# Two decoder layers with a mixture of experts: weights moved in transfers of 2 MB instead of 1 MB, through a ring of 16 slots

## What is computed

```
z = h @ w_in                               # 1024 x 3076, heads: 12 dilated, 4 forgetting
y = concat(rms(dilated attention), rms(forgetting attention)) @ w_out
h = layer_norm(alpha * h + y)
probs = softmax(h @ w_router + b_router)   # 16 experts in 4 groups
# the best group, then the best 2 experts inside it, gates normalised
for every chosen expert e:
    a = silu(x @ w_gate[e]) * (x @ w_up[e]);  out += gate * (a @ w_down[e])
h = layer_norm(alpha * h + out)
```

## Time and profile before

| | us |
|---|---|
| median of three runs | 1417.3 |
| the profiled execution | 1413.33 |
| its span, first to last instruction | 1411.7 |
| PE busy | 1159.9 (82%) |
| VectorE busy | 295.4 (21%) |
| ScalarE busy | 181.0 (13%) |

### The profile page before, as it was taken

One profiled execution on the slowest core, in us unless ns is written; L12 is line 12 of the kernel. 1 busy time (PEld: TensorE's weight loads), 2 busy tenths in 40 slices (PEclk: granted clock), 3 DMA queues, 4 the chain that ended last, 5 costly groups with the idle time before them and its releaser, 6 DMA issues.

```text
span 1411.7 us, 17085 instructions
## 1 busy us (share of the span) xinstructions
PE 1159.9 (82%) x5948; PEld 556.2 (39%) x5949; DVE 295.4 (21%) x777; ACT 181.0 (13%) x407; POOL 4.6 (0%) x12
## 2 busy tenths in 40 slices
PE   7999967799987677777999895989999877567765
PEld 4456453334432323233445644434444323222322
DVE  1334241111111111113235324010202111111113
ACT  1044210001001000000105411000000010000100
POOL 0000000000000000000000000000000000000000
PEclk9999978999999899889799996899999998878998
DMA  9931129999999999999942121647888999999995
GB/s 365 394 120 61 60 90 368 382 417 422 422 421 422 421 422 421 422 423 419 414 148 94 60 92 59 233 146 261 341 357 330 422 422 421 422 421 422 422 421 218
DMA packets 62361, 444.72 MB, mean 315 GB/s; under 512 B 7152, under 2 KB 7408, under 8 KB 8944
## 3 DMA queue, kind: packets, MB, share of 16 engines
q1 hardware_dynamic: 61168, 439.97, 76.7%
q0 software_dynamic: 1152, 4.19, 0.8%
HBM read 443.08 MB, written 1.05 MB: 315 GB/s over the span
## 4 chain that ended last, share of the span: by engine, by line
PE 58%; DMA 30%; issue 6%; DVE 3%; SPq 2%; ACT 1%; DVEq 0%; ACTq 0%
DMA ring<-in_w_up_dram 22%; PE acc L668 12%; PE lo L586 9%; PE lo L486 9%; PE lo L474 8%; DMA ring<-in_w_down_dram 8%; PE acc L746 4%; PE lo L461 3%; SPq L319 2%; PE acc L540 1%; PE acc L391 1%; PE lo L382 1%; PE lo L759 1%; PE lo L437 1%; PE acc L643 1%
## 5 line engine op out<-in xcount | busy, mean ns | idle before, releaser
L486 PE MATMUL lo<-ring,z 128*32 128x512 f32 x2112 | 281.6, 671 | 148.0 <-DMA ring<-in_w_up_dram 107.6
L486 PEld LDWEIGHTS lo<-ring,z 128*32 128x32 f32 x2112 | 65.6, 120 | 343.1 <-issue 158.5
L668 PE MATMUL acc<-ring,actT 128*128 128x512 f32 x384 | 176.1, 616 | 1.5 <-ACT actT L832 1.5
L474 PE MATMUL lo<-ring,z 128*64 128x512 f32 x672 | 152.8, 609 | 24.6 <-issue 22.7
L461 PEld LDWEIGHTS lo<-z,h 128*128 128x128 f32 x1088 | 132.4, 196 | 55.2 <-issue 51.0
L461 PE MATMUL lo<-z,h 128*128 128x128 f32 x1088 | 148.7, 287 | 2.5 <-DVE z L1173 2.5
L586 PE MATMUL lo<-ring,z 128*128 128x512 f32 x288 | 129.2, 610 | 19.9 <-issue 19.9
L668 PEld LDWEIGHTS acc<-ring,actT 128*128 128x128 f32 x384 | 74.7, 199 | 90.5 <-issue 90.5
L474 PEld LDWEIGHTS lo<-ring,z 128*64 128x64 f32 x672 | 48.3, 140 | 123.9 <-issue 113.7
L586 PEld LDWEIGHTS lo<-ring,z 128*128 128x128 f32 x288 | 56.0, 197 | 90.3 <-issue 90.3
L935 ACT ACTIVATE z<-lo 64x512 f32<-64x512 f32 x22 | 13.1, 593 | 493.5 <-PE lo L486 493.5
(11 more groups left out here) (179 smaller groups left out, 712.3 us busy)
## 6 DMA issues: line engine op xcount, KB each, us to landing
ring<-in_w_gate_dram SPq DMA_DIRECT2D x128, 1024.0 KB, 15.9
ring<-in_w_up_dram SPq DMA_DIRECT2D x128, 1024.0 KB, 18.9
ring<-in_w_down_dram SPq DMA_DIRECT2D x128, 1024.0 KB, 25.0
ring<-in_w_in_dram SPq DMA_DIRECT2D x24, 1024.0 KB, 24.7
ring<-in_w_out_dram SPq DMA_DIRECT2D x8, 1024.0 KB, 30.3
ln_gb<-in_ln_dram POOLq DMA_DIRECT2D x8, 512.0 KB, 7.2
cst<-in_consts_dram SPq DMA_DIRECT2D x1, 1416.0 KB, 13.6
h<-in_x_dram SPq DMA_DIRECT2D x1, 1024.0 KB, 5.5
```

The lines of the kernel that those rows point to most:

```text
L474: mm = nc.tensor.matmul(lo[half * W:(half + 1) * W, bank, :], lhsT, ring[:, s, at:at + 512], start=start, stop=stop, skip_group_check=True)
L486: return nc.tensor.matmul(lo[at * T:(at + 1) * T, bank, :], lhsT, ring[:, s, col:col + 512], start=start, stop=stop, skip_group_check=True)
L668: mm = nc.tensor.matmul(acc[:, 2 + t, :], actT[:, k, t * P:(t + 1) * P], ring[:, 2 * c + k // 4, (k % 4) * CH:(k % 4 + 1) * CH], start=(k ...
```

## The change

The host lays the weights out so that 2 MB are contiguous, with 16 KB for each partition, and one transfer fills two neighbouring slots. SP waits for both slots to be free, and signals `ring_full` of the first of them alone. PE waits once for each pair. PE still frees each slot by itself, at the same instruction as before. The 416 weight transfers of 1 MB become 208 of 2 MB; bytes, order, slots and all arithmetic stay.

```diff
-    w_in = np.stack([slots_of(a["w_in"][:, :, c * CH:(c + 1) * CH], 4) for c in range(N_CH)], 1)
+    w_in = np.stack([slots_of(a["w_in"][:, :, c * CH:(c + 1) * CH], KB) for c in range(N_CH)], 1)
-    out = {"x": a["x"], "w_in": w_in, "w_out": slots_of(a["w_out"], 2),
-           "w_gate": slots_of(a["w_gate"], 2), "w_up": slots_of(a["w_up"], 2), "w_down": slots_of(a["w_down"], 2),
+    out = {"x": a["x"], "w_in": w_in, "w_out": slots_of(a["w_out"], 4),
+           "w_gate": slots_of(a["w_gate"], 4), "w_up": slots_of(a["w_up"], 4), "w_down": slots_of(a["w_down"], 4),
...
+            def two_slots(s):
+                return ring[:, s:s + 2, :].rearrange("p s n -> p (s n)")
...
             def load_matrix(layer, m, expert, first, turn):
-                for i in range(4):
-                    s = first + i
+                for i in range(2):
+                    s = first + 2 * i
                     sp.wait_ge(ring_free[s], turn)
+                    sp.wait_ge(ring_free[s + 1], turn)
                     src = expert_v[m][:, bass.ds(layer, 1), bass.ds(expert, 1), i, :]
-                    sp.dma_start(ring[:, s, :], src.rearrange("p l e f -> p (l e f)")).then_inc(ring_full[s], 16)
+                    sp.dma_start(two_slots(s), src.rearrange("p l e f -> p (l e f)")).then_inc(ring_full[s], 16)
...
             def tiny_gate_up(first, gate_full, full):
                 for i in range(4):
-                    pe.wait_ge(ring_full[first + i], gate_full)
-                    pe.wait_ge(ring_full[UP + i], full)
+                    if i % 2 == 0:
+                        pe.wait_ge(ring_full[first + i], gate_full)
+                        pe.wait_ge(ring_full[UP + i], full)
...
                 for s in range(4):
-                    pe.wait_ge(ring_full[DOWN + s], full)
+                    if s % 2 == 0:
+                        pe.wait_ge(ring_full[DOWN + s], full)
```

More of the change, by code:

```diff
@@ L333, in _ @@
                         sp.sem_inc(passed, 1)
[L334 to L340, removed]
+                    s = 2 * c
+                    for i in range(2):
+                        sp.wait_ge(ring_free[s + i], gate_turn if s < UP else turn)
+                    src = w_in_v[:, bass.ds(l, 1), c, 0, :]
+                    sp.dma_start(two_slots(s), src.rearrange("p l n -> p (l n)")).then_inc(ring_full[s], 16)
+                for q in range(2):
+                    s = ODD + 2 * q
+                    for i in range(2):
+                        sp.wait_ge(ring_free[s + i], gate_turn)
                     src = w_out_v[:, bass.ds(l, 1), q, :]
-                    sp.dma_start(ring[:, ODD + q, :], src.rearrange("p l n -> p (l n)")).then_inc(ring_full[ODD + q], 16)
+                    sp.dma_start(two_slots(s), src.rearrange("p l n -> p (l n)")).then_inc(ring_full[s], 16)
                 load_matrix(l, 0, 0, EVEN, sp.snap(gate_turn + 1))
@@ L557, in narrow_item @@
                 for i in range(4):
-                    if i >= 1:
+                    if i == 2:
                         pe.wait_ge(ring_full[UP + i], full)
@@ L665, in project @@
                 for k in ks:
-                    if t == 0 and k % 4 == 0:
-                        pe.wait_ge(ring_full[2 * c + k // 4], fulls[2 * c >= UP])
+                    if t == 0 and k == 0:
+                        pe.wait_ge(ring_full[2 * c], fulls[2 * c >= UP])
                     mm = nc.tensor.matmul(acc[:, 2 + t, :], actT[:, k, t * P:(t + 1) * P],
@@ L740, in _ @@
                     for k in range(KB):
-                        if t == 0 and k % 2 == 0:
+                        if t == 0 and k % 4 == 0:
                             pe.wait_ge(ring_full[ODD + k // 2], gate_full)
```

## The result

| | kernel before | changed kernel | ratio, 95% interval |
|---|---|---|---|
| first comparison, median us | 1415.5 | 1404.1 | 0.9918 (0.9895 to 0.9941) |
| second comparison, median us | 1413.8 | 1405.5 | 0.9936 (0.9914 to 0.9957) |
| profiled execution, us | 1413.3 | 1404.7 | |

The change makes the kernel 0.6 to 0.8% faster: the medians differ by 11.4 us in the first comparison (4 executions of each kernel) and by 8.3 in the second (21 before, 8 changed), where 7.5 were forecast. The second interval holds the forecast's 1409.8 / 1417.3 = 0.9947; the first ends 0.0006 short of it.

The account below looks back on a forecast made before the run. The weights' stream was taken to bound two stretches, with PE setting the time in others. -12.3 + 1.5 + 0.7 + 1.8 + 0.8 = -7.5 us, from the median of 1417.3 to 1409.8 us, range 1402 to 1420.

Parts of the forecast that it names:

- The rate: Both layers' weight streams: 10 ns per packet, 0.089 us saved per pair of slots, 138 pairs, -12.3 us.
- The store and x: Two other transfers used to estimate a packet's own time: 15 ns from the store, some 29 from the load of x.
- the constants: Their 11 KB rows, at 39.8 us per MB against the weights' 38.5, showed no gain from longer rows.
- The start: Where each layer's stream starts, the first pair waits for its second slot: +1.5 us in layer 0, +0.7 in layer 1.
- The start of the kernel: w_in's first two slots go out together at 3 us, before PE has its turned input: costs nothing.
- The end: Each layer's last down matrix: 16 products instead of 8 after the last landing, +0.9 us per layer, +1.8.
- Within an item: Paired waits and freeing inside a stream's items cost 0, unless a lower TensorE clock adds up to 3 us per layer.
- Code fetches: Two places in layer 0 where PE stands for code while DMA is full: longer packets delay it, +0.8 us (0 to 2).
- The sign for a wrong prediction: Wrong if the rate rises and the end of layer 0's experts doesn't move by some 3 us.
- that only signals go: Rival: hardware cuts 16 KB rows into two 8 KB packets, saving 1.4 us against 4.8; 1420.7 us, chance 0.08.
- that 16 KB rows stream worse: Rival: 16 KB rows go at the constants' rate, 138 pairs cost 23.5 us; 1445.6 us, mild form 1429, chance 0.10.
- the small packet time (a = 3.5 ns): Rival: a pair gains only 0.031 us, 4.3 us in all against 4.8 of losses; 1417.8 us, no change, chance 0.17.

Follow-up runs that it names:

- experiment 1: Changed kernel with its 2 MB transfers and paired waits, but in the old rows of 8 KB; 1418.1 us, 1.0033 against the kernel before.
- experiment 2: Kernel before with its 1 MB transfers, but SP and PE both wait for two slots at once; 1418.4 us, 1.0036.
- experiment 6: Changed kernel with gate and down matrices in transfers of 4 MB, up matrices in 2 MB; 1419.9 us, 1.0053 against the kernel before.
- second traces: Traces of two unchanged repeats: the changed kernel once more (ratio 0.9936) and the kernel before once more as a control (1.0000).
- experiment 10: Kernel before with 1 MB transfers and PE's waits per slot, only SP waits for two free slots; ratio 1.0000.
- experiment 7: Changed kernel with the last 2 MB of each layer's last down matrix as two 1 MB transfers, a wait for each; 1406.7 us, 0.9947 against the kernel before.
- experiment 4: Changed kernel with each 4 MB expert matrix in one transfer, rows of 32 KB, waits for four slots; 1447.6 us, 1.0254 against the kernel before.
- experiment 3: Kernel before with its 1 MB transfers and waits per slot, but in rows of 4 KB; 1431.8 us, 1.0130.
- experiment 8: Changed kernel with gate matrices in one transfer of 4 MB, up and down in 2 MB; 1412.3 us, 0.9980 against the kernel before.

## Why the prediction was right

**The rate, -12.3 forecast.** The term was right in kind and about a sixth too large: 0.075 us per pair (4.970 - 4.895) times 138 is -10.4. It can be read a second way, from the changed kernel's items against experiments 1 and 2, which lack its rows: -10.4 and -10.8. The chosen 10 ns per packet were 0.075 / 9 = 8.3 ns, with 9.4 from rows of 4 KB. The store and x were too high with 15 and 29, as suspected for their start, and the constants misleading on the other side.

The Trainium skill ("DMA: Bandwidth & Descriptors", "Where 436 GB/s comes from") puts the ceiling of the SBUF ports at 435 GB/s. The 428 GB/s of the changed kernel and the 431 of experiment 6 lie below it, so no run here shows a ceiling. The Trainium skill's rule of about 3 cycles beside a packet's bytes (same page, "Why small descriptors are slow (HBM only)"), by which an estimated 4 us would have been won against 4.8 of costs, is too small here: 8 KB against 16 KB rows differ by 1.5%, not 0.6%.

**The start, +1.5 and +0.7.** In layer 0 the first pair of the stream was issued at 279.0 and landed after 7.7 us:

```profile
L323 SPq DMA_DIRECT2D ring<-in_w_gate_dram x1: 333/333/333, 279.0 to 279.0; - x1
...
DMA to landing us min/median/max: 7.7/7.7/7.7
```

at 286.7, where 287.1 was forecast; but this execution reached its items 1.2 us earlier. Counted from the first item, the pair landed after 77.9 us and the second slot of the kernel before after 75.6: +2.3 us, where 1.5 were forecast (+2.2 between the second traces). 0.6 of the excess is the landing itself, 7.7 us for a lone pair instead of 4.7 + 2.4; the other 0.2 is PE, which freed the slot later. In layer 1 the pair landed 199.1 us after the first item, and the slot of the kernel before after 199.0:

```profile
L323 SPq DMA_DIRECT2D ring<-in_w_gate_dram x1: 333/333/333, 1067.9 to 1067.9; - x1
...
DMA to landing us min/median/max: 7.6/7.6/7.6
```

That is +0.1 (-0.4 between the second traces), where 0.7 were forecast. Experiment 10 says the same of SP's waits alone: 1.5 in layer 0, nothing in layer 1.

**The start of the kernel, 0.** This term was put at nothing, because w_in's first two slots go out together before PE has its turned input. In the changed kernel they land after PE has it. PE's first projection waits for the pair, where that of the kernel before waits for ScalarE:

```profile
12.93 14.00 PE L680 MATMUL acc<-ring,actT 128*128 128x512 f32 x32 [1.47 <-DMA ring<-in_w_in_dram]
...
12.47 13.99 PE L668 MATMUL acc<-ring,actT 128*128 128x512 f32 x32 [0.76 <-ACT actT L832]
```

The wait is 0.7 us longer (1.12 us in the second trace of the changed kernel, 0.4 longer). It lies outside the items.

**The end, +1.8.** 16 products in 1.92 us after the last wait in both layers instead of 8 in 1.06, as written: +1.7. Experiment 7 puts 8 of them before the last wait again and wins 1.2 and 0.7.

**Within an item, 0.** Held: the DMA share stayed 1.01 to the end of layer 0. What didn't hold is the sign that PE's total wait for DMA would shrink by the gain: it grew, by the pairing of the waits (experiment 2). Experiment 4 shows how near the edge is: with four slots the same wait costs 28 us.

**Code fetches, +0.8.** 7.77 and 7.46 us instead of 7.70 and 7.27 (the second of these from the same view as the earlier trace rows): +0.3, where 0.8 were forecast. Doubled packets hardly delay them. The start in layer 0 holds part of this already, since PE frees that pair after both fetches.

**The sum.** -10.4 + 2.3 + 0.1 + 0 + 1.7 = -6.3, where the fetches' 0.3 is not added, since the 2.3 holds part of it, and the item stages give -5.8 and -6.3. So the forecast's -7.5 had a rate a little too good against costs nearly right in sum, with layer 0's start too small and layer 1's too large. The sign for a wrong prediction, that the end of layer 0's experts doesn't move by some 3 us, can't be read in time from the start: it moved from 660.5 to 657.3 between the first traces and from 661.3 to 661.5 between the second, because what precedes the items varies by 5 us. From the first item on it moved by 2.0 and 2.2.

The whole executions gained more, 8.3 and 11.4 us. The two profiled pairs differ by 8.7 and 8.9 us in span, of which 2.9 and 2.6 lie outside the items. There the change isn't absent, for w_in and w_out come in pairs too, but the only effect found is the cost above. The forecast had nothing won there: that the whole executions gained 7.5 us and more, though the items gave 5.8 to 6.3, is in part luck. One place outside the items is known: layer 1's projection is 4.1 us shorter in both traces of the changed kernel (last section), and kernels with rows of 4 and 8 KB (experiments 3 and 10) have that shorter time too. Whether any of the gain outside the items belongs to the change stays open; both comparisons' intervals (8 to 15 and 6.1 to 12.2 us) lie above 5.8, so I can't call it chance.

The rivals: that only signals go is out by the packet count; that 16 KB rows stream worse is out by the rate; the small packet time (a = 3.5 ns) is out by two measurements.

## What to carry to other kernels

When a stream of weights sets the time and its transfers already hold 1 MB, look at the contiguous row per partition, not at the transfer: in this stream each packet cost some 8 to 9 ns beside its bytes, by the steps from rows of 4 to 8 and from 8 to 16 KB. Each coarsening here was paid where a stream starts and ends, so work out those few microseconds first; and compare how long the consumer holds the last slot with what is then left in the queue, because once that is negative the price comes once per item. A ratio over whole executions could not tell 6 us from 9 here; stages cut at the same instructions repeated within half a microsecond for one kernel, and within about one between two kernels that should be alike.

## What the runs showed of the hardware

The same instructions on the same data took different times from trace to trace. In layer 1's projection (192 products, first and last start) the kernel before took 109.8 us in both of its traces, and the changed one 105.7 in both of its own:

```profile
L668 PE MATMUL acc<-ring,actT x192: 592/592/1216, 676.1 to 785.9; 128*128 128x512 f32 x192
```

```profile
L680 PE MATMUL acc<-ring,actT x192: 592/592/1217, 677.0 to 782.6; 128*128 128x512 f32 x192
```

The difference is TensorE's clock. Before the projection PE is busy a third of the time in both (4.35 us from 664 to 676 before, 4.73 from 660 to 672.9 changed). From 676 to 679 us the kernel before was granted 0.50 of full speed, which is 1.2 GHz, and its products there last 1061 to 1216 ns; from 684 to 690 us it was granted 1.00, 2.4 GHz, and they last 593. The stretch of the whole projection, before and changed:

```profile
676.10:786.50 110.40, 110.05 (x383) 58.17 (x383) 36.91 (x118) 24.74 (x79) 0.00 (x0) 0.95 0.51 196
...
672.90:779.20 106.30, 105.95 (x383) 56.05 (x383) 36.91 (x118) 24.76 (x79) 0.00 (x0) 0.98 0.48 190
```

The kernel before stands at half speed again from 696 to 700 us (0.50), where the changed one has 1.00 (693 to 700 us). A product takes nearly twice as long at half speed, so 4 us more mean some 8 us more at 1.2 GHz. Of the eight other kernels three take 109.6 to 109.9 us (experiments 1, 2 and 7) and five 105.6 to 105.8 (3, 4, 6, 8 and 10), so rows, transfers and waits don't decide it by themselves: experiment 7 differs from the changed kernel only in each layer's last transfer and the waits around it. What does decide it isn't shown. In layer 0's projection even one kernel's two traces differ: 107.2 and 105.8 us before, 105.6 and 107.3 changed.

I had not expected rows to matter above 8 KB as steadily as they do:

```
row     us per MB of stream     GB/s
4 KB    2.560                   410
8 KB    2.485                   422
16 KB   2.448                   428
32 KB   2.43                    431   (between two landings, to about 1%)
```
